# A smaller DMA descriptor scratch for Pool, w_o wholly in SBUF, and a four-block weight ring

## The chip, the cores and the metric

The kernel runs on one core of one Trainium2 chip. The metric is device time in microseconds: the median of the runs of one kernel, on the slowest (here the only) core. Everything is float32.

## The reference, cut to what matters

One layer of a streaming encoder works on 512 new prompt frames and 8 x 16 sample frames of width 1024. It computes `h = x + [retention ; latent attention](RMSNorm(x)) @ w_o`, then `h + PEER(RMSNorm(h))`, then a final RMSNorm. `w_o` is 1024 x 1024. In PEER each token makes 16 query vectors of 128 with `w_q` (1024 x 2048), scores them against 16 x 128 sub-keys, and so picks 16 of 16,384 experts for each of 8 heads. Each pick fetches one row of 1024 floats of `u` and one of `v`:

```
u = take(u_tab, expert)                 # 128 rows of 4 KB per token
a = gelu(einsum('td,thkd->thk', xb, u)) * g
v = take(v_tab, expert)                 # 128 more
out = einsum('thk,thkd->td', a, v)
```

## The kernel before, in words

The 640 tokens are five tiles of 128 (t = 0 to 4; tile 4 holds the sample frames), one token per partition. Tile t goes through retention and attention, then `w_o` (L892), `residual` (L1533), the second norm, `query` (L922), key scores, top-16 searches, and the picks. In tiles 0 and 2, two further tiles are projected with `w_in` at the end (`project`, L687).

**The gathers.** Each of a tile's 128 picks per token is one indirect DMA of 128 rows x 4 KB, once from `u` and once from `v`: 1280 in all, issued by Pool (`gather_u` L642, `gather_v` L652). They land in `rows`, a ring of 13 slots. VectorE takes the dot product of a u slot with the token (`dot`, L1681), TensorE adds a v slot, weighted, into the sum in PSUM (`add_row`, L1012). A slot is gathered into again only when that has been done (`wait_slot`, L632), so at most 13 gathers are under way. The picks of tile t are worked on during tile t+1: `ENDS`, `stages_of` and `slot_units` spread units of two picks between the steps by fixed shares, in the same written order on TensorE, VectorE and ScalarE. After tile 4 only gathers and their work are left.

**The weights.** SyncE (SP) issues, in one fixed order, blocks of 128 x 4 KB into the ring `wblk`, which has `WB` = 3 buffers. A block's DMA waits until the block `WB` before it has been used (`wblk_used`). Six of the eight blocks of `w_o` (`KEPT`) are loaded once into `w_o_kept`. The other two go through the ring in every tile, ahead of the 16 blocks of `w_q`; in tiles 0 and 2, 21 blocks of `w_in` follow (L595). In tile 0, 13 of the `w_q` blocks go by Pool into the 13 row slots instead, which are still free, and three through the ring. `block_base` and `query_block` number the ring's blocks. SP's loads for a tile stand behind its stores of the latent keys of that tile; after the first three, SP also stores the final output of tile t-2 (which waits for that output) and loads the residual `x` into `hbuf` (L570 to L575).

`residual` waits on VectorE for `wblk_used` to count the last `w_o` block. `copy_queries` (L1216) waits on ScalarE for four used query blocks.

Of the kernel before, what the change touches and what calls it, by code (L numbers as in the profile page):

```python
# [13 lines left out]
P = 128  # L14
# [29 lines left out]
IN_BLOCKS = 21  # L44
ST_BUFS = 5
SLOTS = 13
KEPT = 6
HELD = SLOTS
FIRST_ORDER = (4, 5, 0, 1, 2, 3)
LAG = 16  # L50
# [33 lines left out]
FIRST_LEFT = 15  # L84

def block_base(t):

    return t * (KD - KEPT + HP) + IN_BLOCKS * sum(s < t for s in PAIRED) - (HELD if t else 0)

def query_block(t, hp):

    return block_base(t) + KD - KEPT + hp - (0 if t else HELD)

def steps_of(t):
# [145 lines left out]
def build(nc, a, out):  # L243
# [3 lines left out]
    with ctx:  # L247
        def sb(name, shape, dt=F32):
            return ctx.enter_context(nc.sbuf_tensor(name, shape, dt))

        def sem(name):
            return ctx.enter_context(nc.semaphore(name))
# [3 lines left out]

        rows = sb("rows", [P, SLOTS, D_MODEL])
        spread_w = sb("spread_w", [P, 2, ITEMS * ROPE])
        WB = 3
        wblk = sb("wblk", [P, WB, D_MODEL])  # L260
        PJ, MIX, R = 0, 3072, 4096
        work = sb("work", [P, R + 7872])
# [27 lines left out]
        st_buf = [keys_all[0:HD, 512 * i:512 * i + 512] for i in range(ST_BUFS)]  # L290
        state = sb("state", [HD, HEADS, HD])
        hbuf = sb("hbuf", [P, 2, D_MODEL])
        w_o_kept = sb("w_o_kept", [P, KEPT, D_MODEL])
        eidx = sb("eidx", [P, 2, PICKS], U32)
        gate = sb("gate", [P, 2, PICKS])
        pair_idx = sb("pair_idx", [P, 2, PICKS], U32)
# [105 lines left out]
        def weighed(t, step):  # L402

            return max((g + 1 for place, g in WEIGHED_AT.get(t, {}).items() if place[0] in step), default=0)
# [28 lines left out]
        outs_done = sem("outs_done")  # L433
        new_ckv_out = sem("new_ckv_out")
        y_out = sem("y_out")
        kept_in, held_used, win_half = sem("kept_in"), sem("held_used"), sem("win_half")
        sq_done, ms1, root1, rstd1_ok = sem("sq_done"), sem("ms1"), sem("root1"), sem("rstd1_ok")
        xt_ok, mm_in, ev_in = sem("xt_ok"), sem("mm_in"), sem("ev_in")
        xt_pair_ok, ev_pj = sem("xt_pair_ok"), sem("ev_pj")
# [44 lines left out]
        def _(sp):  # L484
# [17 lines left out]
            sp.wait_ge(mm_in, NIN)  # L502
            for t in range(1, TILES):
                sp.dma_start(xs[t], a["x_all"][P * t:P * t + P, :]).then_inc(xs_in[1], 16)
            for k in range(KEPT):
                sp.dma_start(w_o_kept[:, k, :], a["w_o"][P * k:P * k + P, :]).then_inc(kept_in, 16)
            sp.wait_ge(sq_done, 1)
            for tile in range(2):
                sp.dma_start(xt_early[tile], a["x_t"][:, :, P * (tile + 1):P * (tile + 2)]).then_inc(xt_in[1], 16)
# [11 lines left out]
            for t in range(TILES):  # L521
# [45 lines left out]
                            sp.dma_start(ca_n[c % 2], out["ckv_s"][DEC_SEQ * c:DEC_SEQ * c + DEC_SEQ, :]  # L567
                                         ).then_inc(s, 16)

                for at, i in enumerate(i for i in range(KD + HP - KEPT) if t or not KD - KEPT <= i < KD - KEPT + HELD):  # L570
                    if at == WB:
                        if t >= 2:
                            store_y(t - 2)
                            sp.wait_ge(y_out, 48 * (t - 1))
                        sp.dma_start(hbuf[:, t % 2, :], a["x_all"][P * t:P * t + P, :]).then_inc(xres_in, 16)  # L575
                    k = i + KEPT
                    n = block_base(t) + i if k < KD else query_block(t, k - KD)
                    if n >= WB:
                        sp.wait_ge(wblk_used, n - WB + 1)
                    src = a["w_o"][P * k:P * k + P, :] if k < KD else a["w_q"][k - KD]  # L580
                    sp.dma_start(wblk[:, n % WB, :], src).then_inc(wblk_in[n % WB], 16)
                    if t == SAMPLE - 1 and k == KD + 4:
                        sp.wait_ge(ev_pv, (SAMPLE - 1) * HEADS)
                        sp.wait_ge(outs_done, 32 * SAMPLE)
                        for h in range(ST_BUFS):
                            sp.dma_start(st_buf[h], a["state"][h]).then_inc(st_landed[h], 16)
                if t in PAIRED:
                    for b in range(IN_BLOCKS):
                        n = query_block(t, HP) + b
                        sp.wait_ge(wblk_used, n - WB + 1)  # L590
                        if b < IN_BLOCKS - 1:
                            dst, src = wblk[:, n % WB, :], a["w_in"][b // 4, :, D_MODEL * (b % 4):D_MODEL * (b % 4 + 1)]
                        else:
                            dst, src = wblk[:, n % WB, 0:KD * ROPE], a["w_in_pe"]
                        sp.dma_start(dst, src).then_inc(wblk_in[n % WB], 16)  # L595
                        if b == 1 and t:
                            sp.wait_ge(mm_ps, 4 * (t + 1))
                            sp.dma_start(xt_pair, a["x_t"][:, :, P * (t + 1):P * (t + 3)]).then_inc(xt_in[1], 16)
# [9 lines left out]
        def _(pool):  # L608
# [18 lines left out]
            for hp in range(HELD):  # L627
                if hp == 6:
                    pool.wait_ge(mm_pv, HEADS)
                pool.dma_start(row_slot[hp], a["w_q"][hp]).then_inc(row_in[hp], 16)  # L630

            def wait_slot(place):  # L632
                if place < SLOTS:
# [36 lines left out]
        def _(pe):  # L670
# [16 lines left out]
            def project(t, b):  # L687

                p, cb = t // 2, b // 4
                n = query_block(t, HP) + b  # L690
                if b == 0:
                    pe.wait_ge(xt_pair_ok, KD * (p + 2))
                    pe.wait_ge(ev_ps, 4 * (t + 1))
                elif b % 4 == 0:
                    pe.wait_ge(ev_pj, 12 * p + 2 * cb)
                pe.wait_ge(wblk_in[n % WB], 16 * (n // WB + 1))
                ks = range(2 * (b % 4), 2 * (b % 4) + 2) if cb < 5 else range(KD)
                for i, k in enumerate(ks):
                    for tile in range(2):
                        last = mm(F[tile][:, 0:width[cb]], pair_tokens(p, k, tile),  # L700
                                  wblk[:, n % WB, width[cb] * i:width[cb] * i + width[cb]],
                                  start=(k == 0), stop=(k == KD - 1), skip_group_check=True)
                last.then_inc(wblk_used, 1)
# [190 lines left out]
            def w_o(t, i):  # L894
                if i == 0:
                    pe.wait_ge(ev_mix, 2 * (t + 1))
                    if weighed(t, ("attend",)):
                        pe.wait_ge(spread_ok, weighed(t, ("attend",)))
                for k in (2 * i, 2 * i + 1):
                    n = block_base(t) + k - KEPT  # L900
                    if k >= KEPT:
                        pe.wait_ge(wblk_in[n % WB], 16 * (n // WB + 1))
                    elif t == 0:
                        pe.wait_ge(kept_in, 16 * KEPT)
                    held = w_o_kept[:, k, :] if k < KEPT else wblk[:, n % WB, :]
                    for half, bank in ((0, 3), (1, 0)):
                        last = mm(F[bank][:, :], mix_t[:, k, :], held[:, 512 * half:512 * half + 512],  # L907
                                  start=(k == 0), stop=(k == KD - 1), skip_group_check=True)
                    if k >= KEPT:
                        last.then_inc(wblk_used, 1)  # L910

            def turn_x2(t):
                pe.wait_ge(x2_ok, t + 1)
# [8 lines left out]
            def query(t, i):  # L922

                if i == 0:
                    pe.wait_ge(ev_x2, 2 * (t + 1))
                g = i // 2
                bank = 3 if g % 2 == 0 else 0
                if g >= 2 and i % 2 == 0:
                    pe.wait_ge(ev_pq, 4 * t + g - 1)
                if i == 4 and ("query", 3) in WEIGHED_AT.get(t, {}):  # L930
                    pe.wait_ge(spread_ok, weighed(t, ("query",)))
                for hp in (2 * i, 2 * i + 1):
                    n = query_block(t, hp)
                    held = t == 0 and hp < HELD
                    if held:
                        pe.wait_ge(row_in[hp], 16)
                    else:
                        pe.wait_ge(wblk_in[n % WB], 16 * (n // WB + 1))
                    src = row_slot[hp] if held else wblk[:, n % WB, :]
                    for k in range(KD):  # L940
                        last = mm(f4(bank)[:, hp % 4, :], src[:, P * k:P * k + P], x2_t[:, k, :],  # L941
                                  start=(k == 0), stop=(k == KD - 1))
                    last.then_inc(held_used if held else wblk_used, 1)

            def key_scores(t, g):
                if t == 0 and g == 0:
# [134 lines left out]
        def _(act):  # L1081
# [30 lines left out]
            def project(t, cb):  # L1112

                p, w = t // 2, width[cb]
                act.wait_ge(wblk_used, query_block(t, HP) + min(4 * cb + 4, IN_BLOCKS))
                if t == 0 and cb == 0:
                    act.wait_ge(rstd1_ok, 2)
                nc.scalar.activation(pj[:, 512 * cb:512 * cb + w], F[0][:, 0:w], ACT.Copy,
# [97 lines left out]
            def copy_queries(t, g):  # L1216
                if g == 0:
                    act.wait_ge(outs_done, 32 * (t + 1))
                if t == 0:
                    act.wait_ge(held_used, min(4 * g + 4, HELD))  # L1220
                if t or 4 * g + 4 > HELD:
                    act.wait_ge(wblk_used, query_block(t, 4 * g + 4))
                copy(pq_t[:, 4 * g:4 * g + 4, :], f4(3 if g % 2 == 0 else 0)).then_inc(ev_pq, 1)

            def copy_key_scores(t, g):
# [113 lines left out]
        def _(dve):  # L1339
# [192 lines left out]

            def residual(t):  # L1533
                h = hbuf[:, t % 2, :]
                dve.wait_ge(wblk_used, block_base(t) + KD - KEPT)
                dve.wait_ge(xres_in, 16 * (t + 1))
                v.tensor_tensor(h[:, 0:512], h[:, 0:512], F[3][:, :], ALU.add)
                link(v.tensor_tensor(h[:, 512:1024], h[:, 512:1024], F[0][:, :], ALU.add))
# [312 lines left out]
```

## Time and profile before

| what | value |
|---|---|
| time, median of 3 runs | 2014.22 us (2009.98 to 2015.17) |
| span of the profiled execution | 2013.7 us |
| PE / VectorE / Pool / ScalarE busy | 78% / 62% / 61% / 13% |
| moved by DMA | 783.78 MB, mean 389 GB/s |
| of it Pool's own queue | 689.13 MB |
| of it SP's and ScalarE's queue | 90.81 MB |

The page states no time of the profiled execution beside its span; the span lies 0.5 us under the median of the timed runs. "DMA share" is the mean share of time in which the core's 16 DMA engines had packets under way (packets overlap, so it can pass 1), and GB/s is what they moved. A weight block is 512 KB, and so is a gather.

### The profile page before, as it was taken

What the parts mean: (1) busy time and instruction counts of PE and PEld (TensorE: products, weight loads), DVE (VectorE), ACT (ScalarE), POOL (GpSimd) and SP (SyncE); (2) the same over time, 40 slices, a digit from 0 to 9 for tenths busy, and PEclk for the clock granted to TensorE, in tenths of its full rate; (3) what the DMA queues carried; (4) which work ended last, traced back from release to release, by engine and by line L of the source; (5) the groups of instructions that cost most, each with busy time, mean ns of one, the idle gap of its engine ahead of it and who ended that gap; (6) DMA issues with size and microseconds to landing.
All of it is one profiled execution on the core that took longest, in us unless ns stands there. A gap on an engine that the chain in (4) does not pass through costs nothing.

```text
span 2013.7 us, 18853 instructions
## 1 busy us (share of the span) xinstructions
PE 1571.0 (78%) x6519; PEld 634.4 (32%) x6519; DVE 1252.4 (62%) x3207; ACT 253.0 (13%) x568; POOL 1233.9 (61%) x1307
## 2 busy tenths in 40 slices
PE   8988879885798868896898776879888666666677
PEld 4573434450333532232353430224445000000000
DVE  2459886399865585548565498885447964544430
ACT  2310122110121111011221000112201000000000
POOL 1114575656767565557667567766665677677774
PEclk9789878896899989898898876888988666666679
DMA  7649999999999999999999999999999999999998
GB/s 297 252 155 411 409 385 401 410 396 377 398 409 410 409 406 410 409 400 397 409 410 409 395 409 409 392 387 396 401 409 409 409 408 409 408 409 409 409 410 320
DMA packets 223742, 783.78 MB, mean 389 GB/s; under 512 B 26816, under 2 KB 33856, under 8 KB 222496
## 3 DMA queue, kind: packets, MB, share of 16 engines
q0 software_dynamic: 187280, 689.13, 86.4%
q1 hardware_dynamic: 34640, 90.81, 11.7%
q10 hardware_dynamic: 1728, 2.65, 0.4%
q8 instruction: 51, 0.84, 0.2%
q14 instruction: 43, 0.35, 0.0%
HBM read 775.31 MB, written 7.19 MB: 389 GB/s over the span
## 4 chain that ended last, share of the span: by engine, by line
DMA 32%; PE 28%; DVE 18%; POOL 14%; issue 6%; ACT 1%; SPq 0%; DVEq 0%; POOLq 0%; ACTq 0%
DMA rows<-in_v,pair_idx 22%; PE acc L1012 8%; POOL rows L658 7%; POOL rows L648 7%; DVE rows L1681 7%; DMA rows<-in_u,eidx 6%; PE F L700 4%; PE F L941 3%; PE F L907 3%; DMA wblk<-in_w_q 2%; PE F L872 1%; PE acc L683 1%; PE F L827 1%; DVE work L1557 1%; DVE work L1565 1%
## 5 line engine op out<-in xcount | busy, mean ns | idle before, releaser
L1012 PE MATMUL acc<-rows,spread_w 128*32 128x512 f32 x2560 | 792.4, 748 | 329.1 <-DMA rows<-in_v,pair_idx 328.2
L1681 DVE CUSTOM_DVE_ANT_0 rows<-rows,xps 128x1024 f32<-128x1024 f32 x640 | 764.8, 1219 | 451.8 <-DMA rows<-in_u,eidx 449.5
L648 POOL DMA_INDIRECT rows<-in_u,eidx x640 | 610.3, 954 | 389.6 <-PE acc L1012 167.0
L658 POOL DMA_INDIRECT rows<-in_v,pair_idx x640 | 609.4, 952 | 282.6 <-issue 156.4
L1012 PEld LDWEIGHTS acc<-rows,spread_w 128*32 128x32 f32 x2560 | 112.7, 120 | 891.8 <-DMA rows<-in_v,pair_idx 742.9
L941 PE MATMUL F<-work,wblk 128*128 128x128 f32 x1072 | 147.4, 299 | 21.2 <-DMA wblk<-in_w_q 19.1
L941 PEld LDWEIGHTS F<-work,wblk 128*128 128x128 f32 x1072 | 138.4, 211 | 53.2 <-issue 29.7
L700 PE MATMUL F<-wblk,work 128*128 128x512 f32 (+1 forms) x192 | 81.5, 573 | 2.7 <-ACT work L1122 2.7
L1554 DVE MAX8 work<-work 128x8 f32<-128x128 f32 (+1 forms) x120 | 25.9, 271 | 59.2 <-ACT work L1227 58.9
L700 PE MATMUL F<-wblk,hbuf 128*128 128x512 f32 (+1 forms) x96 | 46.9, 571 | 17.5 <-ACT work L1122 16.7
L907 PE MATMUL F<-w_o_kept,work 128*128 128x512 f32 x120 | 57.3, 627 | 2.9 <-ACT work L1209 2.9
L1681 DVE DVE_READ_ACCUMULATOR2_ANT dots<- 128x1 f32 x640 | 52.7, 82 | 0.0
L700 PEld LDWEIGHTS F<-wblk,work 128*128 128x128 f32 x192 | 34.4, 201 | 50.8 <-issue 44.8
L1692 DVE COPY stat<-stat 32x1 f32<-32x1 f32 x20 | 2.9, 145 | 72.3 <-ACT hbuf L1257 72.1
L827 PE MATMUL F<-keys_all,work 128*128 128x128 f32 (+3 forms) x128 | 45.3, 481 | 1.1 <-ACT work L1142 0.7
L700 PE MATMUL F<-wblk,lnf 128*128 128x512 f32 (+1 forms) x96 | 45.7, 559 | 0.0
L1249 ACT COPY spread_w<-F 32x32 f32<-32x32 f32 x80 | 16.6, 207 | 218.2 <-PE F L985 217.5
L626 POOL MEMSET spread_w<- 128x2048 f32 x1 | 1.8, 1832 | 61.8 <-DVE ssq L1378 61.8
L872 PE MATMUL F<-work,keys_all 128*128 128x128 f32 x288 | 38.5, 284 | 0.5 <-ACT work L1183 0.5
L872 PEld LDWEIGHTS F<-work,keys_all 128*128 128x128 f32 x288 | 33.9, 191 | 15.6 <-issue 14.9
L907 PEld LDWEIGHTS F<-w_o_kept,work 128*128 128x128 f32 x120 | 22.9, 199 | 34.6 <-issue 30.6
L1236 ACT ACTIVATE dots<-dots 128x32 f32<-128x32 f32 x20 | 4.6, 229 | 231.7 <-DVE dots L1681 231.6
(276 smaller groups left out, 1451.2 us busy)
## 6 DMA issues: line engine op xcount, KB each, us to landing
wblk<-in_w_q SPq DMA_DIRECT2D x67, 512.0 KB, 7.5
wblk<-in_w_in SPq DMA_DIRECT2D x40, 512.0 KB, 6.8
rows<-in_u,eidx POOLq DMA_INDIRECT x640, 11.2
rows<-in_v,pair_idx POOLq DMA_INDIRECT x640, 11.5
rows<-in_w_in POOLq DMA_DIRECT2D x4, 2048.0 KB, 11.8
rows<-in_w_q POOLq DMA_DIRECT2D x13, 512.0 KB, 8.2
wblk<-in_w_o SPq DMA_DIRECT2D x10, 512.0 KB, 10.9
w_o_kept<-in_w_o SPq DMA_DIRECT2D x6, 512.0 KB, 9.8
```

The lines of the kernel that those rows point to most:

```text
L648: nc.gpsimd.indirect_dma_start(row_slot[u_place(n) % SLOTS], None, a["u"], bass.IndirectOffsetOnAxis(eidx[:, t % 2, pick:pick + 1], 0)).th ...
L658: nc.gpsimd.indirect_dma_start(row_slot[v_place(n) % SLOTS], None, a["v"], bass.IndirectOffsetOnAxis(pair_idx[:, t % 2, item:item + 1], 0) ...
L683: last = mm(banks[o % 4][:, 0:width[cb]], xt[:, k, :], win[buf][:, k, :], start=(k == 0), stop=(k == KD - 1))
L700: last = mm(F[tile][:, 0:width[cb]], pair_tokens(p, k, tile), wblk[:, n % WB, width[cb] * i:width[cb] * i + width[cb]], start=(k == 0), st ...
L827: mm(dst[:, 0:nk], qlat[:, k, u, :], ckvt[:, k, 0:nk], start=(k == 0), stop=False)
L872: last = mm(F[3][:, P * k:P * k + P], lhs, prob_t[u % 2][0:w, P * j:P * j + P], start=(j == 0), stop=(j == len(pieces(t)) - 1))
L907: last = mm(F[bank][:, :], mix_t[:, k, :], held[:, 512 * half:512 * half + 512], start=(k == 0), stop=(k == KD - 1), skip_group_check=True)
L941: last = mm(f4(bank)[:, hp % 4, :], src[:, P * k:P * k + P], x2_t[:, k, :], start=(k == 0), stop=(k == KD - 1))
L1012: last = mm(acc[lo:lo + ROPE, 512 * c:512 * c + 512], spread_w[:, g % 2, at:at + ROPE], row_slot[v_place(q) % SLOTS][:, 512 * c:512 * c + ...
L1554: last = v.max(vals[:, i, 0:8], values_of(i))
L1557: v.max_index(idx[:, i, 0:8], vals[:, i, 0:8], values_of(i))
L1681: v.tensor_tensor_reduce(row_slot[at % SLOTS], row_slot[at % SLOTS], xps[:, :], 1.0, 0.0, ALU.mult, ALU.add, dots[:, g % 2, k:k + 1]).then ...
```

## The change

The descriptor scratch shrinks by 12 KB per partition. The room goes to three blocks of 4 KB per partition: all eight `w_o` blocks stay in SBUF (`w_o_all`), and the weight ring has four buffers. The ring carries `w_q` and `w_in` only. A constant `Q_KEPT` is 0, so the branches that would keep `w_q` blocks are never taken. `residual` waits for a semaphore of the `w_o` step.

```diff
-KEPT = 6
+Q_KEPT = 0
-def block_base(t):
-    return t * (KD - KEPT + HP) + IN_BLOCKS * sum(s < t for s in PAIRED) - (HELD if t else 0)
+def ring_first(t):
+    return Q_KEPT + (0 if t else HELD)
+def ring_base(t):
+    return sum(HP - ring_first(s) + (IN_BLOCKS if s in PAIRED else 0) for s in range(t))
 def query_block(t, hp):
-    return block_base(t) + KD - KEPT + hp - (0 if t else HELD)
+    return ring_base(t) + hp - ring_first(t)
+def in_block(t, b):
+    return query_block(t, HP) + b
...
-        WB = 3
+        WB = 4
-        w_o_kept = sb("w_o_kept", [P, KEPT, D_MODEL])
+        w_o_all = sb("w_o_all", [P, KD, D_MODEL])
...
-            for k in range(KEPT):
-                sp.dma_start(w_o_kept[:, k, :], a["w_o"][P * k:P * k + P, :]).then_inc(kept_in, 16)
+            for k in range(KD):
+                sp.dma_start(w_o_all[:, k, :], a["w_o"][P * k:P * k + P, :]).then_inc(w_o_in, 16)
...
-                for at, i in enumerate(i for i in range(KD + HP - KEPT) if t or not KD - KEPT <= i < KD - KEPT + HELD):
-                    if at == WB:
+                for hp in range(ring_first(t), HP):
+                    if hp == ring_first(t) + (WB if t else 0):
                         if t >= 2:
                             store_y(t - 2)
                             sp.wait_ge(y_out, 48 * (t - 1))
                         sp.dma_start(hbuf[:, t % 2, :], a["x_all"][P * t:P * t + P, :]).then_inc(xres_in, 16)
-                    k = i + KEPT
-                    n = block_base(t) + i if k < KD else query_block(t, k - KD)
+                    n = query_block(t, hp)
                     if n >= WB:
                         sp.wait_ge(wblk_used, n - WB + 1)
-                    src = a["w_o"][P * k:P * k + P, :] if k < KD else a["w_q"][k - KD]
-                    sp.dma_start(wblk[:, n % WB, :], src).then_inc(wblk_in[n % WB], 16)
+                    sp.dma_start(wblk[:, n % WB, :], a["w_q"][hp]).then_inc(wblk_in[n % WB], 16)
...
             def w_o(t, i):
+                    if t == 0:
+                        pe.wait_ge(w_o_in, 16 * KD)
                 for k in (2 * i, 2 * i + 1):
-                    n = block_base(t) + k - KEPT
-                    if k >= KEPT:
-                        pe.wait_ge(wblk_in[n % WB], 16 * (n // WB + 1))
-                    elif t == 0:
-                        pe.wait_ge(kept_in, 16 * KEPT)
...
+                if i == 3:
+                    last.then_inc(mm_wo, 1)
...
             def residual(t):
-                dve.wait_ge(wblk_used, block_base(t) + KD - KEPT)
+                dve.wait_ge(mm_wo, t + 1)
...
-    nc = _bacc.Bacc("TRN2", target_bir_lowering=False, num_devices=1)
+    nc = _bacc.Bacc("TRN2", target_bir_lowering=False, num_devices=1, dynamic_dma_scratch_size=4096)
```

## Rows read from the trace of the kernel before

**Rows 1.** The page: GB/s in 40 slices, and DMA totals.
```profile
GB/s 297 252 155 411 409 385 401 410 396 377 398 409 410 409 406 410 409 400 397 409 410 409 395 409 409 392 387 396 401 409 409 409 408 409 408 409 409 409 410 320
DMA packets 223742, 783.78 MB, mean 389 GB/s; under 512 B 26816, under 2 KB 33856, under 8 KB 222496
q0 software_dynamic: 187280, 689.13, 86.4%
```

**Rows 2.** Windows of stages: PE, PEld, DVE, ACT, POOL busy us, clock, DMA share, GB/s.
```profile
60.00:154.00 94.00, 83.95 (x452) 62.12 (x453) 52.02 (x221) 24.05 (x66) 17.72 (x24) 0.82 0.58 222
150.00:200.00 50.00, 41.50 (x96) 17.25 (x94) 48.73 (x177) 2.76 (x5) 24.56 (x27) 0.99 1.03 410
285.00:435.00 150.00, 132.39 (x740) 76.33 (x739) 87.22 (x254) 28.03 (x68) 90.78 (x97) 0.92 1.02 403
435.00:541.00 106.00, 68.55 (x272) 20.24 (x271) 101.37 (x278) 11.23 (x20) 72.46 (x75) 0.74 1.00 389
541.00:730.00 189.00, 163.02 (x853) 85.52 (x854) 114.53 (x313) 32.89 (x74) 123.62 (x131) 0.93 1.03 409
1428.00:1545.00 117.00, 96.79 (x496) 52.17 (x492) 61.83 (x166) 12.49 (x26) 71.71 (x77) 0.91 1.03 408
1545.00:1990.00 445.00, 298.63 (x837) 42.39 (x835) 229.51 (x503) 14.98 (x43) 325.70 (x345) 0.70 1.03 409
```

**Rows 3.** Waits of TensorE and VectorE for DMAs: us, times, longest.
```profile
DVE rows L1681 <- DMA rows<-in_u,eidx: 449.5, 299, 4.3
PE acc L1012 <- DMA rows<-in_v,pair_idx: 328.2, 329, 4.4
PEld F L941 <- DMA wblk<-in_w_q: 23.4, 19, 2.8
```

**Rows 4.** DMA issues: form, count, KB each, median us to landing.
```profile
wblk<-in_w_q SPq DMA_DIRECT2D x67, 512.0 KB, 7.5
rows<-in_u,eidx POOLq DMA_INDIRECT x640, 11.2
rows<-in_v,pair_idx POOLq DMA_INDIRECT x640, 11.5
wblk<-in_w_o SPq DMA_DIRECT2D x10, 512.0 KB, 10.9
w_o_kept<-in_w_o SPq DMA_DIRECT2D x6, 512.0 KB, 9.8
```

**Rows 5.** SP's DMA issues in order of time: start us, us, what.
```profile
73.90 0.91 SPq L581 DMA_DIRECT2D wblk<-in_w_o  x2
74.86 0.49 SPq L581 DMA_DIRECT2D wblk<-in_w_q  x1
...
141.58 87.07 SPq L595 DMA_DIRECT2D wblk<-in_w_in  x20
...
285.92 0.91 SPq L581 DMA_DIRECT2D wblk<-in_w_o  x2
286.87 0.43 SPq L581 DMA_DIRECT2D wblk<-in_w_q  x1
...
370.13 58.01 SPq L581 DMA_DIRECT2D wblk<-in_w_q  x15
```

**Rows 6.** The chain that ended last, pieces of tiles 0 to 2.
```profile
87.87 16.76 PE F L907 x32
...
385.78 8.11 DMA wblk<-in_w_q
...
401.39 6.66 DMA wblk<-in_w_q
...
679.10 6.79 DMA wblk<-in_w_q
```

**Rows 7.** Windows of 10 us with less than the full rate.
```profile
250.00:260.00 10.00, 10.00 (x71) 6.69 (x69) 9.97 (x18) 5.22 (x7) 6.35 (x7) 1.00 0.83 283
410.00:420.00 10.00, 9.00 (x69) 5.77 (x68) 8.17 (x20) 2.00 (x6) 6.59 (x7) 1.00 0.95 339
490.00:500.00 10.00, 4.46 (x11) 1.05 (x11) 9.70 (x23) 0.83 (x4) 5.73 (x6) 0.66 0.86 284
```

**Rows 8.** Pool's gathers one by one, and all of 1650 to 1990 by line.
```profile
1649.26 0.94 POOL L648 DMA_INDIRECT rows<-in_u,eidx  x1 [0.30 <-issue]
1650.50 0.94 POOL L658 DMA_INDIRECT rows<-in_v,pair_idx  x1 [0.30 <-issue]
...
L658 POOL DMA_INDIRECT rows<-in_v,pair_idx x158: 935/941/950, 1650.5 to 1988.9; - x158
L648 POOL DMA_INDIRECT rows<-in_u,eidx x111: 935/941/942, 1649.3 to 1928.7; - x111
```

More of the change, by code:

```diff
@@ L435, in build @@
         y_out = sem("y_out")
-        kept_in, held_used, win_half = sem("kept_in"), sem("held_used"), sem("win_half")
+        w_o_in, held_used, win_half = sem("w_o_in"), sem("held_used"), sem("win_half")
+        q_kept_in, q_kept_used = sem("q_kept_in"), sem("q_kept_used")
         sq_done, ms1, root1, rstd1_ok = sem("sq_done"), sem("ms1"), sem("root1"), sem("rstd1_ok")
@@ L575, in _ @@
                         sp.dma_start(hbuf[:, t % 2, :], a["x_all"][P * t:P * t + P, :]).then_inc(xres_in, 16)
-                    k = i + KEPT
-                    n = block_base(t) + i if k < KD else query_block(t, k - KD)
+                    n = query_block(t, hp)
                     if n >= WB:
                         sp.wait_ge(wblk_used, n - WB + 1)
-                    src = a["w_o"][P * k:P * k + P, :] if k < KD else a["w_q"][k - KD]
-                    sp.dma_start(wblk[:, n % WB, :], src).then_inc(wblk_in[n % WB], 16)
-                    if t == SAMPLE - 1 and k == KD + 4:
+                    sp.dma_start(wblk[:, n % WB, :], a["w_q"][hp]).then_inc(wblk_in[n % WB], 16)
+                    if t == SAMPLE - 1 and hp == 6:
                         sp.wait_ge(ev_pv, (SAMPLE - 1) * HEADS)
@@ L588, in _ @@
                     for b in range(IN_BLOCKS):
-                        n = query_block(t, HP) + b
-                        sp.wait_ge(wblk_used, n - WB + 1)
+                        n = in_block(t, b)
+                        if n >= WB:
+                            sp.wait_ge(wblk_used, n - WB + 1)
                         if b < IN_BLOCKS - 1:
@@ L629, in _ @@
                     pool.wait_ge(mm_pv, HEADS)
-                pool.dma_start(row_slot[hp], a["w_q"][hp]).then_inc(row_in[hp], 16)
+                pool.dma_start(row_slot[hp], a["w_q"][Q_KEPT + hp]).then_inc(row_in[hp], 16)
             def wait_slot(place):
@@ L689, in project @@
                 p, cb = t // 2, b // 4
-                n = query_block(t, HP) + b
+                n = in_block(t, b)
                 if b == 0:
@@ L898, in w_o @@
                         pe.wait_ge(spread_ok, weighed(t, ("attend",)))
+                    if t == 0:
+                        pe.wait_ge(w_o_in, 16 * KD)
                 for k in (2 * i, 2 * i + 1):
-                    n = block_base(t) + k - KEPT
-                    if k >= KEPT:
-                        pe.wait_ge(wblk_in[n % WB], 16 * (n // WB + 1))
-                    elif t == 0:
-                        pe.wait_ge(kept_in, 16 * KEPT)
-                    held = w_o_kept[:, k, :] if k < KEPT else wblk[:, n % WB, :]
                     for half, bank in ((0, 3), (1, 0)):
-                        last = mm(F[bank][:, :], mix_t[:, k, :], held[:, 512 * half:512 * half + 512],
+                        last = mm(F[bank][:, :], mix_t[:, k, :], w_o_all[:, k, 512 * half:512 * half + 512],
                                   start=(k == 0), stop=(k == KD - 1), skip_group_check=True)
-                    if k >= KEPT:
-                        last.then_inc(wblk_used, 1)
+                if i == 3:
+                    last.then_inc(mm_wo, 1)
             def turn_x2(t):
@@ L933, in query @@
                     n = query_block(t, hp)
-                    held = t == 0 and hp < HELD
-                    if held:
-                        pe.wait_ge(row_in[hp], 16)
+                    if hp < ring_first(t):
+                        pe.wait_ge(row_in[hp - Q_KEPT], 16)
+                        src, used = row_slot[hp - Q_KEPT], held_used
                     else:
                         pe.wait_ge(wblk_in[n % WB], 16 * (n // WB + 1))
-                    src = row_slot[hp] if held else wblk[:, n % WB, :]
+                        src, used = wblk[:, n % WB, :], wblk_used
                     for k in range(KD):
@@ L942, in query @@
                                   start=(k == 0), stop=(k == KD - 1))
-                    last.then_inc(held_used if held else wblk_used, 1)
+                    last.then_inc(used, 1)
             def key_scores(t, g):
@@ L1114, in project @@
                 p, w = t // 2, width[cb]
-                act.wait_ge(wblk_used, query_block(t, HP) + min(4 * cb + 4, IN_BLOCKS))
+                act.wait_ge(wblk_used, in_block(t, min(4 * cb + 4, IN_BLOCKS)))
                 if t == 0 and cb == 0:
@@ L1218, in copy_queries @@
                     act.wait_ge(outs_done, 32 * (t + 1))
[L1219 to L1222, printed above, removed]
+                last = 4 * g + 3
+                if last < Q_KEPT:
+                    act.wait_ge(q_kept_used, Q_KEPT * t + last + 1)
+                elif last < ring_first(t):
+                    act.wait_ge(held_used, last - Q_KEPT + 1)
+                else:
+                    act.wait_ge(wblk_used, query_block(t, last) + 1)
                 copy(pq_t[:, 4 * g:4 * g + 4, :], f4(3 if g % 2 == 0 else 0)).then_inc(ev_pq, 1)
```

## The prediction

> **What bounds the kernel now.** I read the page's rate line first. From the fourth slice on (about 150 us) nearly every slice shows 409 or 410 GB/s, whatever the tile is doing, and none is higher than 411; only the first 150 us run at 155 to 297 [rows 1]. That flat ceiling is the DMA limit. The windows by stage say the same: 541 to 730 us has a DMA share of 1.03 and 409 GB/s while PE is busy 163 of 189 us and VectorE 115, and 1545 to 1990 us, gathers alone, has 409 GB/s with PE at 299 of 445 [rows 2]. Then the waits: VectorE stands 449.5 us and PE 328.2 us for gathered rows, against 23.4 us for `w_q` blocks [rows 3]. So from about 150 us to 1990 us the time is bytes over the rate, plus what is lost where the rate dips. I take 409.5 GB/s as full rate. A block or a gather of 512 KB (524,288 bytes) costs 1.28 us of it.
>
> The exceptions are stretches where VectorE has no room: 150 to 200 us (48.7 of 50 us busy, and still 410 GB/s) and 435 to 541 us (101.4 of 106, 389 GB/s) [rows 2]. The dips lie at the ends of such stretches: 283 GB/s at 250 and 284 at 490, with VectorE at 9.97 and 9.70 of 10 us [rows 7]. There the 13 slots are full of rows that nobody takes.
>
> **The bytes removed.** Before, `w_o` is moved by 10 ring loads and 6 kept loads, 16 blocks [rows 4]; after, by 8. Tile 0 needs all 8 in both kernels, so the eight that go are two in each of tiles 1 to 4. In tile 1 they are issued at 285.92 us, beside a saturated DMA [rows 5, 2]; the pattern repeats in tiles 2, 3 and 4, four such pairs in all. 8 x 524,288 = 4.194 MB, and at 409.5 GB/s that is **10.24 us**. SP's own issue time (0.91 us for two) is hidden, since SP mostly waits.
> The ends for this term: all of it comes back as time, 10.24 us, if the stretches that follow the four loads stay DMA-bound; nothing comes back if a stretch turns out to be bound by an engine. The stretches after the loads have room: VectorE is busy 87 of 150 us at 285 to 435, 115 of 189 at 541 to 730, 62 of 117 at 1428 to 1545; PE 132 of 150, 163 of 189 and 97 of 117, so it has 18, 26 and 20 us to give where 2.56 is asked [rows 2]. I take the full 10.24.
> The Trainium skill ("DMA: Bandwidth & Descriptors", Specifications) puts a core's share of HBM at about 358 GB/s. The trace disagrees with 409.5 GB/s [rows 1, 2]. By the page's figure the term would be 11.7 us, an estimate; the measured rate is used.
>
> **The fourth ring buffer.** (a) In tile 0 the ring before holds w_o6, w_o7 and one `w_q` block at 74.86 us, and the first `w_in` block goes out only at 141.58 us [rows 5]. After, three `w_q` blocks and the first `w_in` block are numbers 0 to 3 and wait for nothing, so that `w_in` block moves into 60 to 154 us, where only 222 GB/s are used [rows 2]. One block less must be moved after 150 us: at most 1.28 us, at least nothing, as VectorE fills 150 to 200 us anyway. I take the middle, 0.6.
> (b) At the query stage only one `w_q` block was ready at its start, two more were asked for while `w_o` freed its buffers (from 370.13 us [rows 5]), and the chain then shows PE standing 8.11, 6.66 and 6.79 us for blocks [rows 6]. After, four are ready at the start. But while PE stands there, the DMA mostly runs at full rate, so PE's time alone brings nothing. What does count is the dip behind it: 410 to 420 us at 339 GB/s loses (409.5 - 339)/409.5 x 10 = 1.7 us [rows 7]; it is the only clear one of its kind. Ends: nothing and 1.7 us; I take 0.9.
> (c) At the head of tiles 1 to 4 four blocks are issued where three were (two `w_o`, one `w_q`). Rows come 1.28 us later there and three blocks fewer (3.84 us) are asked in the query stage: the saving arrives after a small debt. If PE or VectorE takes one such delay into a stretch with no room, it stays. Ends: nothing, and 4 x 1.28 = 5.1 us lost; nearest to the low end, since rows 2 shows PE and VectorE with room in those stretches. I charge 1.0.
>
> **Waits and order.** The `w_o` step of tile 0 now waits for eight blocks, all ahead of `x_t`, `ln2` and `subk` on SP. Before, the last two went out at 73.90 us with 10.9 us to land, so about 85 us; the step starts at 87.87 [rows 4 to 6]. Two blocks more ahead of `x_t`, `ln2` and `subk` delay those by 2.6 us at full rate; the first user is `norm2`, behind the 16.76 us of `w_o` [rows 6]. Cost nothing; without that cover 2.6 us. SP's wait for the output of tile t-2 stands behind four blocks in place of three; queued behind it are the residual's `x` and the fifth `w_q` block, needed only after `w_o` and the first query block. `residual` waits for the same last matmul under another name: nothing.
>
> **Pool's scratch.** The trace doesn't show a small scratch, so this is bounded. A gather takes Pool 0.94 us plus 0.30 us of issue, 1.244 us from start to start [rows 8], against 1.28 us on the DMA: in gather-only stretches Pool has 0.036 us to spare per gather. Below, a shorter scratch can't make a gather faster than its 0.94 us, and Pool isn't the limit, so no gain. What is under way at once is set by the 13 slots. Pool's queue moved 187,280 packets for 1302 DMAs (1280 gathers, 22 loads), 9 per engine and DMA [rows 1, 4]; 13 slots make at most 117 per engine. A quarter of the old room would have to be smaller than that to block. Over 269 gathers in a row the longest takes 0.950 us against a median of 0.941 [rows 8], so nothing periodic is visible in the larger ring in 2421 packets per engine. I take nothing; the upper end is the third rival.
> The Trainium skill ("DMA: Bandwidth & Descriptors", Terms) makes a descriptor 16 bytes in a ring in SBUF. That would be 1024 per engine before and 256 after, 28 gathers instead of 113: above 117, and the old ring would have turned twice within those 269 gathers without a trace. By that rule too the term is nothing, unless Pool halts at a turn, which no row shows.
>
> **The sum.** 10.24 + 0.6 + 0.9 - 1.0 = 10.7 us off. The profiled span is 2013.7, the median of the runs 2014.2; what lies around the span doesn't change. 2014.2 - 10.7 = **2003.5 us**. Its own range is 2000 to 2007.
>
> **Rivals.**
> 1. *The saving turns into waiting for VectorE* (same). The written order ties the units of two picks to steps. If rows arrive sooner, VectorE or PE may become the bound and the DMA rate dips more, as at 250 and 490 us [rows 7]. For it: 101.4 of 106 us at 435 to 541. Against: the freed bytes lie in the stretches with room. It needs 4.7 of the 10.7 us lost to become "same"; with half lost, 5.3, the time is 2009.
> 2. *The deeper ring also closes dips* (more gain). The pieces of the chain that wait for `w_q` blocks are 7 to 8 us each, and a PE that is in time frees slots sooner. The 36 slices from the fourth to the 39th fall short of 409.5 by about 200 GB/s in sum; a slice is 50.3 us, so that is 200/409.5 x 50.3 = 25 us [rows 1], of which most is VectorE's. If a third comes back, 8 us, the time is 1995. Against: VectorE's share in rows 7.
> 3. *Pool pauses at each turn of the small scratch* (slower). Mechanism: before writing over the oldest part of the ring Pool waits for an earlier gather to land. No pause shows in 269 gathers of the larger ring [rows 8], so if turns cost a pause, its turn is longer than 269, and a quarter of it longer than 67: at most 1302/67 = 19 turns. The slack of one turn is 67 x 0.036 = 2.4 us, and from a longer pause on it decides. If Pool waits for the newest gather (landing 11.5 us [rows 4]), that is 19 x (11.5 - 2.4) = 173 us, a time near **2177**. If it waits for one issued 9 or more before (11.5/1.28), that has landed and it costs nothing. Against: by the 13 slots Pool has already seen the gather 13 before land. By the 28 gathers to a turn that the Trainium skill makes ("DMA: Bandwidth & Descriptors", Terms) there would be 46 turns and 483 us, an estimate.
> 4. *The change doesn't do what it says*: if the room weren't there the kernel would not build; if `w_o` were still reloaded, MB moved would stay at 783.8 and the time 2014. I give it nothing of its own; it is in "same".
>
> **Chances.** Forecast 0.64, rival 1 0.18, rival 2 0.10, rival 3 0.08. About 0.3% (6 us) is what a measurement of this kernel can tell from no change. Faster 0.74, same 0.18, slower 0.08. The range of 8 in 10 goes from 1998, which leaves out half of rival 2, to 2012.5, which leaves out the worst of rival 1 and all of rival 3.
>
> **What would show it.** Right: 779.6 MB moved, `w_o` in 8 loads; 409 GB/s in the same stretches, each of tiles 1 to 4 ending about 2.6 us sooner than the one before; the 0.94 us gathers unchanged with no pause at equal distances; waits for `w_q` blocks well under 23 us; the stretch 1545 to 1990 as long as before (445 us) and only shifted. Wrong: gathers above 1 us at equal distances; more windows under 400 GB/s with VectorE full; a gather-only tail longer than before.

## The result, and the profile after

The changed kernel takes **2004.54 us** (median of 4 runs, 2003.82 to 2005.67) against 2013.97 before. The ratio is 0.9956, 95% interval [0.9942, 0.9970]: 6 to 12 us faster, 2003.5 forecast. Timed once more beside other kernels (e9 below) it gave 0.9951 [0.9938, 0.9963].

The page of the kernel after: rates in 40 slices, DMA totals, Pool's queue.

```profile
GB/s 298 278 136 411 409 376 409 400 409 379 395 409 410 409 405 410 410 385 395 409 410 409 393 409 409 397 380 396 405 409 409 409 410 409 407 410 409 409 410 320
DMA packets 222590, 779.59 MB, mean 389 GB/s; under 512 B 26688, under 2 KB 33728, under 8 KB 221344
q0 software_dynamic: 187280, 689.13, 86.7%
```

Beside [rows 1]: 4.19 MB less in all, Pool's queue the same, and the same ceiling of 409 to 411 GB/s. The slices from the fourth to the 39th fall short of 409.5 by 213 GB/s in sum; before it was 199. Times a slice and over 409.5 that is 26.1 us lost (213 x 50.1/409.5), after 24.5 before (199 x 50.3/409.5). The dips did not shrink in this execution. A second profiled execution of the same kernel (e9) gives 31.0 us, so this sum differs by some 5 us between executions of one kernel, and a change of 1.6 us in it says nothing.

DMA issues after (count, KB, median us to landing), and SP's issues in order of time:

```profile
wblk<-in_w_q SPq DMA_DIRECT2D x67, 512.0 KB, 8.1
rows<-in_u,eidx POOLq DMA_INDIRECT x640, 11.0
rows<-in_v,pair_idx POOLq DMA_INDIRECT x640, 11.6
w_o_all<-in_w_o SPq DMA_DIRECT2D x8, 512.0 KB, 10.1
```

```profile
76.89 1.55 SPq L590 DMA_DIRECT2D wblk<-in_w_q  x3
78.49 140.06 SPq L605 DMA_DIRECT2D wblk<-in_w_in  x20
...
285.70 1.86 SPq L590 DMA_DIRECT2D wblk<-in_w_q  x4
287.61 0.42 SPq L586 DMA_DIRECT2D hbuf<-in_x_all  x1
385.79 31.93 SPq L590 DMA_DIRECT2D wblk<-in_w_q  x12
```

Against [rows 4, 5]: `w_o` in 8 loads for 16; the first `w_in` block goes out at 78.49 us instead of 141.58; four blocks stand at the head of tile 1. SP issues the first blocks of tiles 1 to 4 at 285.70, 536.95, 943.33 and 1420.26 us; before it was 285.92, 541.22, 946.08 and 1427.92. So the saving at these heads is 0.2, 4.3, 2.8 and 7.7 us: it builds up from tile to tile, as forecast, though not in even steps of 2.6. Pool's gathers between 1640 and 1980 us, and windows (PE, PEld, DVE, ACT, POOL busy, clock, DMA share, GB/s):

```profile
L668 POOL DMA_INDIRECT rows<-in_v,pair_idx x158: 935/941/950, 1640.3 to 1979.1; - x158
L658 POOL DMA_INDIRECT rows<-in_u,eidx x110: 937/941/955, 1641.5 to 1918.7; - x110
```

```profile
250.00:260.00 10.00, 10.00 (x71) 6.69 (x69) 9.97 (x18) 5.22 (x7) 6.55 (x7) 1.00 0.67 229
285.00:435.00 150.00, 135.25 (x769) 77.51 (x768) 91.33 (x270) 28.59 (x69) 92.62 (x99) 0.92 1.02 407
435.00:541.00 106.00, 68.46 (x253) 18.16 (x251) 99.34 (x264) 11.25 (x22) 73.50 (x76) 0.74 0.99 388
...
410.00:420.00 10.00, 8.28 (x57) 5.31 (x56) 9.75 (x41) 1.17 (x2) 7.57 (x9) 1.00 1.02 407
370.00:380.00 10.00, 5.36 (x28) 2.51 (x27) 7.85 (x14) 0.53 (x2) 6.14 (x7) 0.83 1.00 376
```

The gathers are as before [rows 8]. The last `v` gather of all starts at 1980.8 us against 1990.2 before (both lie just behind the windows of these rows). The dip at 410 us has gone (339, [rows 7], to 407), and the one at 250 us is deeper (283, [rows 7], to 229); both come back in every trace of a ring of four, as e2 shows below. The rest of the stretch varies from execution to execution: 285 to 435 us has 407 GB/s here against 403 [rows 2], but 394 in e9, and the window at 370 us has 376 here and 399 in e9.

### The profile page after: what moved, and what is told of

Same layout as the page of the kernel before. It is cut to its first block, busy times and chain, and to the rows that moved or that the text cites. A ratio compares the mean times of both kernels' runs of the same rounds, so it can differ in the third digit from the quotient of the medians.

```text
span 2003.9 us, 18844 instructions
## 1 busy us (share of the span) xinstructions
PE 1562.3 (78%) x6519; PEld 631.9 (32%) x6519; DVE 1251.9 (62%) x3207; ACT 252.8 (13%) x568; POOL 1231.3 (61%) x1307
## 4 chain that ended last, share of the span: by engine, by line
DMA 29%; PE 28%; DVE 18%; POOL 17%; issue 7%; ACT 1%; SPq 0%; DVEq 0%; ACTq 0%; POOLq 0%
DMA rows<-in_v,pair_idx 22%; POOL rows L658 8%; PE acc L1018 8%; POOL rows L668 8%; DVE rows L1690 7%; DMA rows<-in_u,eidx 6%; PE F L710 4%; PE F L913 3%; PE F L947 2%; PE F L882 1%; PE acc L693 1%; DVE work L1574 1%; DVE work L1566 1%; PE F L837 1%; DVE work L1626 1%
## 5 line engine op out<-in xcount | busy, mean ns | idle before, releaser
L947 PEld LDWEIGHTS F<-work,wblk 128*128 128x128 f32 x1072 | 130.4, 202 | 30.0 <-issue 28.1
L947 PE MATMUL F<-work,wblk 128*128 128x128 f32 x1072 | 136.5, 288 | 2.5 <-issue 2.0
L913 PE MATMUL F<-w_o_all,work 128*128 128x512 f32 x160 | 77.5, 635 | 2.8 <-ACT work L1215 2.8
L913 PEld LDWEIGHTS F<-w_o_all,work 128*128 128x128 f32 x160 | 31.1, 202 | 46.8 <-issue 42.7
## 6 DMA issues: line engine op xcount, KB each, us to landing
rows<-in_v,pair_idx POOLq DMA_INDIRECT x640, 11.6
```

Of the source, the lines that this page charges most:

```text
L913: last = mm(F[bank][:, :], mix_t[:, k, :], w_o_all[:, k, 512 * half:512 * half + 512], start=(k == 0), stop=(k == KD - 1), skip_group_chec ...
```

## The experiments

Every ratio is to the kernel before, timed in the same set. Times are medians.

| label | what | us | ratio [95%] |
|---|---|---|---|
| (after) | the change | 2004.5 | 0.9956 [0.9942, 0.9970] |
| e1 | before, scratch 4 KB | 2014.5 | 0.9998 [0.9990, 1.0007] |
| e2 | after, ring of 3 | 2007.6 | 0.9961 [0.9947, 0.9976] |
| e3 | after, reload 2 w_o blocks a tile | 2017.4 | 1.0013 [1.0002, 1.0024] |
| e4 | after, reload 6 | 2033.8 | 1.0096 [1.0080, 1.0111] |
| e5 | one w_q block kept, ring of 3 | 2000.9 | 0.9942 [0.9927, 0.9957] |
| e6 | two kept, ring of 2 | 2032.4 | 1.0106 [1.0086, 1.0127] |
| e7 | after, scratch 2 KB | 2004.0 | 0.9955 [0.9942, 0.9967] |
| e8 | after, scratch 1088 B | 2010.8 | 0.9997 [0.9984, 1.0010] |
| e9 | after, once more | 2005.4 | 0.9951 [0.9938, 0.9963] |
| e10 | e3, reload issued in the dips | 2009.4 | 0.9967 [0.9955, 0.9979] |
| e11 | e5, first blocks issued in the dips | 1993.2 | 0.9885 [0.9869, 0.9902] |
| e12 | after, first blocks issued in the dips | 1997.0 | 0.9916 [0.9902, 0.9930] |

**e1, the scratch alone.** The kernel before with `dynamic_dma_scratch_size=4096`.

> The kernel before with a 4 KB scratch and nothing else. My theory: the scratch costs nothing and gives nothing, 2014 us within 3 us, gathers still 0.941 us in the median. Rival (Pool pauses at turns of the scratch, hidden in the changed kernel by the bytes saved): 2016 to 2030 us. Rival (a smaller scratch is itself a gain): under 2010.

0.9998 [0.9990, 1.0007]. The scratch neither costs nor gives anything at 4 KB; it only makes room. The rivals fall. Over the whole span some gathers do take longer than the 0.95 us of [rows 8]: of 1280, those of 1.05 us or more number 42 before, 38 after and 45 in e1. 31 of e1's 45 have the same number in the order of issue as in the kernel before, whose scratch is four times as large, so they do not go by turns of the scratch.

**e2, the ring of three.**
```diff
-        WB = 4
+        WB = 3
```

> The changed kernel with the ring back at three buffers; all eight w_o blocks stay. My theory: only bytes count, so it keeps 10.2 us less the 0.6 and 0.9 of the fourth buffer: about 2005 to 2006 us against 2004.5. Rival (the fourth buffer is where the gain comes from, since PE's waits for w_q blocks went from 23 us to none): 2010 to 2014, with PE waiting some 20 us for w_q again.

0.9961 [0.9947, 0.9976] against 0.9956 and 0.9951 for the ring of four; the 2007.6 us lie between the forecast and the rival's range, and the ratio decides for the forecast. PE waits for `w_q` as before the change (us, times, longest):

```profile
PEld F L947 <- DMA wblk<-in_w_q: 23.7, 20, 2.6
PE F L947 <- DMA wblk<-in_w_q: 18.9, 18, 2.4
```

In the kernel after these lines are:

```profile
PEld F L947 <- DMA wblk<-in_w_q: 1.9, 4, 0.8
PE F L947 <- DMA wblk<-in_w_q: 0.4, 2, 0.2
```

So the fourth buffer takes away nearly all of PE's waits for weights, and the time hardly notices: 0.0005 to 0.0010, 1 to 2 us, inside the intervals.

What it does to the dips shows in tile 1, in GB/s of two windows. Each line holds every traced kernel of its kind that issues its blocks in the old order:

| ring | kernels | 250 to 260 us | 410 to 420 us |
|---|---|---|---|
| three | before, e1, e2, e5 | 283, 273, 286, 274 | 339, 336, 334, 331 |
| four | after, e9, e7, e8, e3, e4 | 229, 259, 197, 232, 240, 220 | 407, 408, 409, 408, 407, 409 |

The fourth buffer does close the dip at 410 us and deepens the one at 250. At 250 us Pool stands about as long in both kinds for a slot that VectorE frees (9.1 us in e2, 8.9 in the kernel after), so the slots are not the difference. A likely one is that the ring of four has its last `w_in` block issued 10 us sooner (78.49 + 140.06 = 218.6 us against 141.58 + 87.07 = 228.7 [rows 5]), so that fewer weights are left to fill that pause. e5 fits: it has a ring of three, issues its first `w_in` block early too (79.72 us), but its last at 228.2, and has the dip of a ring of three. No run tested that reading on its own.

**e3 and e4, the bytes back.** Blocks of `w_o` are loaded again into their own place; n is 2 or 6.
```diff
+                if t:
+                    sp.wait_ge(mm_wo, t)
+                    for k in range(KD - n, KD):
+                        sp.dma_start(w_o_all[:, k, :], a["w_o"][P * k:P * k + P, :]).then_inc(w_o_in, 16)
                 for hp in range(ring_first(t), HP):
...
-                    if t == 0:
-                        pe.wait_ge(w_o_in, 16 * KD)
+                    pe.wait_ge(w_o_in, 16 * (KD + n * t))
```

> The changed kernel, but w_o blocks 6 and 7 are loaded again into their own place at the head of tiles 1 to 4: the bytes of before (8 more blocks, 783.8 MB) with a ring of four. My theory: 8 x 1.28 = 10.2 us more than the changed kernel, 2014 to 2015. Rival (the gain is the ring's or PE's, bytes are hidden): 2004 to 2007.

> The same with six w_o blocks loaded again in tiles 1 to 4, 24 blocks more than the changed kernel. My theory, time is bytes over 409.5 GB/s: 24 x 1.28 = 30.7 us more, 2033 to 2036. Rival (the stretches at the heads of the tiles have slack that hides part): under 2025.

e3, with the bytes of before and the ring of after, is as slow as before or a trace slower, and 2.4 us over its forecast range; e4 is 1.40% over the kernel after (1.0096 - 0.9956), 28 us for 24 blocks or 1.18 us a block; from e3 to e4 it is 1.04. From the kernel after to e3 it is 11.5 us for 8. The four steps, with e2's, lie between 1.0 and 1.4 us a block, around the 1.28 of the rate. A difference of two ratios is uncertain by some 0.002 (4 us), which is 0.5 us a block where 8 blocks differ and 0.2 where 24 do. "Bytes are hidden" falls.

**e5 and e6, more weights kept.** `w_q` blocks below `Q_KEPT` are loaded once into a tile of their own, which the ring pays for.
```diff
-Q_KEPT = 0
+Q_KEPT = 1          # e6: 2
...
-        WB = 4
+        WB = 3          # e6: 2
+        w_q_kept = sb("w_q_kept", [P, Q_KEPT, D_MODEL])
...
+            for hp in range(Q_KEPT):
+                sp.dma_start(w_q_kept[:, hp, :], a["w_q"][hp]).then_inc(q_kept_in, 16)
```

> The changed kernel with the room of the fourth ring buffer given to one w_q block that stays in SBUF (ring of three). Four blocks less to move than in the changed kernel. Byte theory: 4 x 1.28 = 5.1 us less, plus at most 1.5 for the ring: 1999 to 2001 us. Rival (a ring of three makes PE wait and gives the gain back): 2004 to 2008.

> Two w_q blocks stay and the ring has two buffers; eight blocks less than in the changed kernel. Byte theory alone: 1994 to 1996 us. Rival: a ring of two can't cover a landing time of 7 to 8 us (PE needs a block each 3 us or so in the query stage), PE waits, slots come free late and the DMA rate dips in the query stages: 2000 us or more, with waits for w_q blocks over 50 us. I hold the rival for likelier here.

e5 beats the changed kernel by its point value, 0.9942 to 0.9956: 2.8 us where 5.1 less the ring were expected, and the intervals overlap. e6 is 0.0164 over e5, 33 us, although it moves 2.1 MB less. Its waits for blocks, what Pool and VectorE wait for between 250 and 290 us, and two of its windows:

```profile
PE F L954 <- DMA wblk<-in_w_q: 65.4, 29, 7.4
PEld F L713 <- DMA wblk<-in_w_in: 44.8, 23, 4.5
```

```profile
POOL rows L671 <- DVE dots L1697: 34.5, 1, 34.5
DVE pair_idx L1667 <- PE F L977: 30.2, 1, 30.2
```

```profile
250.00:290.00 40.00, 36.45 (x187) 20.29 (x189) 20.28 (x36) 7.77 (x15) 10.82 (x12) 0.91 0.47 170
420.00:450.00 30.00, 24.89 (x173) 20.54 (x175) 20.49 (x85) 2.94 (x8) 11.26 (x12) 0.89 0.83 301
```

At 250 to 290 us the DMA moves 170 GB/s. Pool stands 34.5 us for a slot that a dot product of VectorE frees, and VectorE, idle half the window, stands 30.2 us for a transpose of PE (L977). PE is busy 36 of the 40 us; I read that as work that its waits for `w_in` blocks have put off. This is the depth at which the ring matters: three buffers hide PE's waits under a full DMA, two don't.

**e7 and e8, a still smaller scratch.** 2048 and 1088 bytes.

> The changed kernel with a scratch of 2 KB. My theory: what must fit is what is under way, 13 gathers of 9 packets per engine; by the Trainium skill's 16 bytes (DMA: Bandwidth & Descriptors, Terms) 2 KB would hold 128. Same time as the changed kernel, 2004.5 within 3 us. Rival (Pool pauses at each turn, and turns are now twice as many): slower by 3 us or more, with gathers over 1 us at equal distances.

> The changed kernel with a scratch of 1088 bytes, about a quarter of the changed kernel's. If room is in proportion, it holds about 7 gathers where up to 13 are under way. My theory: Pool now has to wait for a gather to land before it writes the next one's descriptors; gathers get longer (median above 1.1 us), fewer are under way, and the time goes up, 2020 to 2300 us, as the rate falls under 409. Rival (the DMA stays full with 7 under way, since 7 x 1.28 = 9 us is near the landing time without a backlog): within 5 us of the changed kernel, with shorter landing times (7 to 9 us) and longer gathers on Pool. Rival (the scratch is not what limits): nothing changes at all.

e7 is the kernel after again (0.9955). e8 loses 0.0041, about 8 us (6.8 between the medians of e8 and e7), less than the least I gave and a little more than the first rival did. Pool's gathers in e8 one by one, then the landing times and a window of e8:

```profile
1704.21 0.94 POOL L658 DMA_INDIRECT rows<-in_u,eidx  x1 [0.33 <-issue]
1705.50 0.94 POOL L668 DMA_INDIRECT rows<-in_v,pair_idx  x1 [0.35 <-issue]
1706.78 0.94 POOL L658 DMA_INDIRECT rows<-in_u,eidx  x1 [0.34 <-issue]
```

```profile
rows<-in_u,eidx POOLq DMA_INDIRECT x640, 8.5
rows<-in_v,pair_idx POOLq DMA_INDIRECT x640, 8.5
```

```profile
1650.00:1700.00 50.00, 32.05 (x80) 3.43 (x76) 23.73 (x40) 0.23 (x1) 36.98 (x40) 0.64 1.03 409
```

Now most gathers start 1.27 to 1.29 us apart, the DMA's own pace, and not 1.244 [rows 8]. On the average the pace was 1.28 us before too (1.28 over 197 gathers from 1600 us on in the kernel after, 1.29 in e8), but there Pool runs at 1.244 and then stands up to 4 us for a slot; now it is paced by landings, one by one. 8.5 us to landing over 1.28 makes about 7 under way, where 11.0 to 11.6 us made 9. The median instruction isn't longer; the wait stands in the gap before it, put down to "issue". My theory was right that Pool would wait and wrong that the rate would fall: 7 under way still fill the DMA, as the first rival said, though the longer gathers that both expected did not come. Where the 8 us go the record does not show. In e8's rates in 40 slices

```profile
GB/s 298 256 147 407 410 367 409 392 409 380 396 409 410 409 405 409 409 398 382 408 410 409 393 409 403 401 398 395 403 400 409 402 398 409 410 410 409 409 410 329
```

the same sum over slices gives 30.2 us lost to dips, inside the 26.1 to 31.0 of the two executions of the kernel after. That with fewer rows ahead each hold-up of VectorE or PE reaches the DMA sooner is a guess that no run tested.

**e9 to e12, where the bytes are moved.** If only a full DMA makes bytes dear, blocks issued in a dip should be cheap. SP waits for `qk_ok`, which falls due at 249, 498, 897 and 1253 us in the kernel after, instead of behind the stores of the latent keys (and in tile 4 the loads of the caches). That is 37, 39, 46 and 167 us sooner than in the kernel after, not the 31 to 80 of the expectation. The first three times lie at or near dips; the fourth lies ahead of smaller ones (313 GB/s at 1320). e11 and e12 issue their `w_q` blocks there, e10 its two `w_o` blocks; the loop behind leaves them out.
```diff
             for t in range(TILES):
+                if t:
+                    sp.wait_ge(qk_ok, t + 1)
+                    for hp in range(ring_first(t), ring_first(t) + WB):     # e10: w_o blocks 6 and 7
+                        load_query(t, hp)
```

> The changed kernel itself, timed beside the other three of this set for a tighter comparison. My theory: 2003 to 2006 us, 8 to 11 us under the kernel before.

> As the run that reloads two w_o blocks in tiles 1 to 4, but SP issues them when the rotated queries and keys are ready: in the changed kernel's trace at 249, 498, 897 and 1253 us, where the DMA rate dips, instead of 31 to 80 us later. Same 783.8 MB. If bytes moved in a dip are free (theory: time is bytes over the rate only where the DMA is full), most of the 10 us disappears: 2005 to 2009 us. Rival (a byte costs the same wherever it is issued): 2014 to 2017, as the run with the reload behind the latent keys.

> One w_q block kept, ring of three, and SP issues the first three w_q blocks of tiles 1 to 4 in the dip (when the rotated queries and keys are ready) instead of behind the stores of the latent keys. Dips lose some 26 us in all; 12 blocks (15.4 us of DMA time) are moved into them. If a third to a half fits: 5 us or so under the same kernel with the old order (2000.9), 1994 to 1998. Rival (the dips are there because slots are full, and the blocks only push the next gathers back by as much): 2000 to 2003.

> The changed kernel with the first four w_q blocks of tiles 1 to 4 issued in the dip. Same bytes as the changed kernel. If dips take bytes for free: 1997 to 2001 us. Rival: 2003 to 2006.

e10 moves e3's bytes and costs 0.0016 over e9 in the same set (3 us), where e3 cost 0.0057 over the kernel after (11.5 us). e12 moves the bytes of the kernel after and takes 0.0035 off it (7 us; the intervals don't overlap), and e11 is the fastest of all: 0.9885 [0.9869, 0.9902], 22 to 23 us under the kernel before and 8 (by medians) to 12 us (by ratios) under e5. e10 and e11 lie 0.4 and 0.8 us outside the ranges expected. What Pool stands for between 245 and 265 us in the kernel after, and windows; then the same of e12:

```profile
POOL rows L668 <- DVE dots L1690: 8.9, 1, 8.9
```

```profile
245.00:285.00 40.00, 28.46 (x149) 12.74 (x148) 37.86 (x71) 5.63 (x9) 25.46 (x27) 0.76 0.94 363
890.00:910.00 20.00, 14.50 (x77) 6.25 (x73) 16.53 (x30) 5.22 (x7) 10.77 (x12) 0.93 0.83 305
```

```profile
POOL rows L676 <- DVE dots L1698: 8.9, 1, 8.9
```

```profile
245.00:285.00 40.00, 27.66 (x152) 12.93 (x147) 37.42 (x70) 6.04 (x11) 26.86 (x28) 0.80 1.02 403
890.00:910.00 20.00, 14.08 (x64) 8.43 (x63) 12.48 (x22) 4.78 (x7) 14.40 (x16) 0.68 1.02 406
```

```profile
GB/s 300 284 140 412 406 410 409 406 409 376 410 409 410 409 405 410 410 405 396 409 410 409 395 409 408 403 394 396 404 409 409 400 396 409 410 409 409 409 410 323
```

The dips of 363 and 305 GB/s fill to 403 and 406, while Pool stands the same 8.9 us for a slot: what fills the dip is the weight blocks. By the last row, e12's rates in 40 slices, the sum over slices is 143 GB/s: 17.4 us lost, where the four traces with a ring of four, the same bytes and the old order (after, e9, e7, e8) have 26.1, 31.0, 26.8 and 30.2.

## Why the prediction was right, step by step

The forecast of 2003.5 us is 1 us off. That is closer than a measurement of this kernel can tell (the interval is 6 us wide): the term of the bytes, 10.24 of the 10.7 us, carries it, and the three small terms sum to 0.5 us, which no run can separate from nothing.

- **Bytes: 10.24 us.** Right in kind, and in size within the intervals: taking 8 blocks away alone (e2) gave 0.9961, 7.9 us [4.8, 10.7], and putting them back (e3) took 11.5. The premise "bytes over the rate where the DMA is full" is shown from both sides, by e3, e4 and e10.
- **First `w_in` block, 0.6 us.** It moved into the unfilled start as said (78.49 us). Its time was not measured alone. The prediction asked only whether VectorE fills 150 to 200 us; it had nothing for the dip at 250 us, which is deeper in every ring of four. From 245 to 285 us the kernel after has 363 GB/s and before has 375, 12 x 40/409.5 = 1.2 us more lost. That is about what this term could bring at most (1.28), so the two together are worth nothing that shows.
- **The ring closes the dip at 410 us, 0.9 us.** The dip went, in all six traces of the table under e2, and PE's waits with it, 1.7 us by the upper end of the forecast. Whether the sum of all dips moved can't be seen: it is 24.5 us before and 29.2 in e1, 26.1 after and 31.0 in e9. So this term is right in kind and not measured in size. Together with the debt of 1.0 charged for the heads of the tiles, the fourth buffer was put at 0.5 us net; e2 against the kernel after gives 1 to 2 us with an interval that holds 0.
- **The debt at the heads of the tiles, 1.0 us.** No run isolates it.
- **Waits and order: nothing.** Right: the `w_o` step of tile 0 starts at 87.85 us against 87.87.
- **How the two profiles close.** Bytes 10.24, the earlier `w_in` block up to 1.28, dips 1.6 more: 9.9 us. The spans differ by 9.8 (2013.7 to 2003.9). This is no proof, since bytes over the rate plus what the slices fall short make up the span of any execution.
- **Scratch: nothing.** Right (e1, e7), and for the reason given: it must hold what is under way. e8 shows the mechanism of the third rival, but not its place or price: Pool waits for one landing at each gather, not at a turn, and it costs 8 us, not 173.
- **The tail.** The saving was there when tile 4's queries ended and was only carried on. The last `w_q` block is used at 1545.5 us after:

```profile
L947 PEld LDWEIGHTS F<-work,wblk x1072: 186/192/338, 139.3 to 1545.5; 128*128 128x128 f32 x179
```

against 1556.3 in the same row of before. From there to the last gather's start it is 435.3 us after and 433.9 before.
- **Rivals.** The first needed 4.7 us of the saving lost to VectorE; the ratios 0.9956 and 0.9951 are 9 to 10 us, and no trace shows a loss to VectorE that stands out from what two executions differ by. The "deeper ring closes dips" rival was wrong in its 8 us: a ring of four closes the dip at 410 us (at most 1.7 us) and deepens another. It was right that the dips can be had, by another means: the moment of issue (e12).

What stays open: why e3 is a trace slower than e1 (1.0013 to 0.9998) with the same bytes and a deeper ring (the intervals just overlap), why the dip at 250 us is deeper with a ring of four, and where e8's 8 us go.

## What to carry to other kernels

Where the rate line is flat at its ceiling, count bytes: each one taken away is worth its time at that rate, and an engine's short waits for data under it (here up to 2.8 us each, 23.4 us in all [rows 3]) are worth almost nothing. Where the line dips, look at what stands in the queues just then: issuing the same blocks 37 to 167 us sooner, the first three times into a dip that the slots of the gathers could not fill, was worth 7 us (e12), nearly as much as the 8 to 10 us of taking eight blocks away. Before reading a small change of the dips, compare two executions of one kernel: here they differ by 5 us. A reserve such as the scratch, or one more ring buffer, should be sized by what is under way, and no larger; here the room was worth somewhat more as kept weights (e11 0.9885 against e12 0.9916; e5 against the kernel after stays inside the intervals).

## What the runs showed of the hardware

- One core moved 409 to 412 GB/s, mostly from HBM with 4 KB rows, both with gathers alone (409 from 1545 to 1990 us) and with gathers and blocks mixed (410 or 411 from 150 to 200 us); no slice of a fortieth of the span in any traced kernel shows more than 412.
- Pool's scratch for descriptors can be a quarter or an eighth of its default with no change of time (e1 0.9998 to the kernel before; e7 0.9955, the kernel after 0.9956), with 13 slots for gathers of 128 rows. At 1088 bytes some 7 fit, the wait shows as some 0.03 to 0.05 us more of "issue" before most gathers, and 7 in flight still gave 409 GB/s, with 8.5 us to landing instead of 11.0 to 11.6.
